# Transposed input read from memory, and the first three weight pieces split by parts, at the head of a one-core transformer kernel

## The chip, the core and the metric

The kernel runs on one core of a Trainium2 chip. A core has a matrix engine (TensorE: its matmuls are PE in the rows, its weight loads PEld), VectorE (DVE), ScalarE (ACT), GpSimd (POOL) and SyncE (SP, which here only issues transfers), each with an instruction stream of its own that runs in order and waits on semaphores. Sixteen DMA engines move data between the memory and the core's SBUF. The metric is device microseconds (us) of one execution; lower is better.

## What is computed

Two transformer blocks over 256 tokens of 1024 features, in float32. The part that the change touches is the very beginning, the root-mean-square norm and the first projection:

```python
def rmsnorm(x, g, eps=NORM_EPS):
    xf = x.astype(jnp.float32)
    y = xf * lax.rsqrt(jnp.mean(xf * xf, axis=-1, keepdims=True) + eps)
    return (y * g.astype(jnp.float32)).astype(x.dtype)
...
        h = rmsnorm(x, norm_mix_g[i])
        u = h @ w_in[i]
        u_rwkv, u_attn, u_gate = jnp.split(u, [RWKV_COLS, RWKV_COLS + ATTN_COLS], axis=-1)
        o_a = rwkv7_time_mix(u_rwkv, rwkv_mu[i], rwkv_w0[i], rwkv_w2[i], rwkv_a0[i],
...
    w = -jax.nn.softplus(-(f32(w0) + jnp.tanh(wd) @ f32(w2))) - 0.5
```

Everything behind it (a recurrence over time, attention, the feed-forward layers, the second block) is left as it is.

## The kernel before

**Weights as a stream of pieces.** All weight matrices are cut into 231 pieces of 128 x 2048 floats (1 MB). SyncE loads piece j into `raw[j % 3]`; ScalarE rounds it to the matmul's format into `hi` (emitted by `emit_hi`, a CAST at L2649); VectorE computes the remainder `lo = raw - hi` (emitted by `emit_lo`, L3017). A product is made of three matmuls, hi times high part of the activations (L2131), hi times their low part (L2132), lo times the high part (L2133). Piece j + 3 may be loaded when `lo` of piece j is done (`next_raw`, L3623). In the first stage each piece has 8 row blocks (k) and 256 columns, so it is 48 matmuls of 128x256.

**The first norm.** `x` is loaded by tokens into `X` (four transfers of 256 KB, `load_x`, L3627). TensorE transposes it (`n_part`, L2307), VectorE multiplies by the gain `g` out of PSUM (L3093), ScalarE rounds to `HH` (L2666), VectorE forms the remainder `HL` (L3099). The division by each token's root mean square is not applied to `h`: ScalarE sums the squares (`stat`, L2677), GpSimd takes the root (`root`, L3596 to L3602), VectorE puts it on a diagonal (`diag`, L3103 and L3104), TensorE spreads it over all partitions (`n_rows`, L2320, two instructions that the trace shows as four), VectorE copies it to `RB` (L3107), and each piece's result is multiplied by `RB` when it is read from PSUM (`shift`, L3148).

**The first piece.** Piece 0 comes in two halves; `first_piece` runs its matmuls in three parts (L2159, L2160, L2165, L2169). Ahead of them TensorE runs matmuls on zeros and on the identity that compute nothing (`warm`, L2138): 8 on zeros at its start, 9 on the identity (18 in the trace) ahead of piece 0.

**Where the norm's first use ends.** The mixer that eats piece 0 needs, one after another: `RB`, the multiplication L3148 (VectorE), L2696 and L2697 (ScalarE), L3152 and L3153 (VectorE), a table load and tanh (L2701), a table load and sigmoid (L2702, ScalarE), and then matmuls with `small` (L2334 and L2335, TensorE), which stand in the middle of piece 3's matmuls. `small` (the little weights, 1 MB) and the constants from column 256 on are one semaphore, `const_in`.

**What sets the order.** A planner writes one script ahead of time: `emit` adds an instruction with its expected cost to a clock per engine, and an instruction is put behind what is expected to be ready. Each engine then runs its part of the script in that order. So another cost at the beginning can give another order later.

Of the kernel before, what the change touches and what calls it, by code (L numbers as in the profile page):

```python
# [220 lines left out]
def program(nc, ws, xin, pin, colsin, constin, smallin, rowin, out):  # L221
# [4 lines left out]
    with ExitStack() as ctx:  # L226
# [14 lines left out]
        first_raw = sem("first_piece_half_in")  # L241
        first_hi = sem("first_piece_half_hi")
        first_lo = sem("first_piece_half_lo")
# [79 lines left out]
        names = [0]  # L323

# [94 lines left out]

        BK0 = Arena(8 * 4 * S)([128, 2, 512])  # L420
# [265 lines left out]
        def first_piece(c, needs, evac):  # L686

            piece_check("w_in", 0, 0, c)
            yield from split(0)
            yield from room(1)  # L690
            sl = take()
            for part in range(3):
                cur[0] = max(cur[0], lo_due[0] if part == 2 else h_due[1, part])
                emit("first", pe=16 * 0.12, part=part, slot=sl, need=unmet(needs(4 * min(part, 1))))
                if part < 2:
                    yield "pe"
            piece_done(0, sl)
            if not evac(sl, c, NSPL):
                give(sl)
            yield "pe"  # L700
# [389 lines left out]

        class FinalNorm(Norm):
# [148 lines left out]
        nm = Norm("norm_mix_g", table=False)  # L1240
        nm.part(0, 0)
        nm.part(1, 0)
        nm.low(0, 0)
        nm.low(1, 0)
        emit("first_hi")
        nm.part(0, 1)
        nm.part(1, 1)
        emit_hi(0)
        nm.low(0, 1)
        nm.low(1, 1)  # L1250
        emit("first_lo")
        emit_lo(0)
# [429 lines left out]
        def mixers_fill(nm):  # L1682
            for p, c in enumerate(RWKV_ORDER):
                def shift(sl, c, nxt, p=p):
                    early.append((p, c, sl, cur[0]))
                    if p == 1:
                        nm.rows()
                    if p:
                        to_shift.extend(early)
                        early.clear()  # L1690
# [3 lines left out]
                if p == 0:  # L1694
                    yield from first_piece(c, nm.h_needs, shift)
                else:
                    yield from cols_piece("w_in", 0, c, "h", nm.h_needs, shift)
# [414 lines left out]
        def tensor_program(e):  # L2112
# [22 lines left out]
            def warm(sl, n, w, x):  # L2135

                for _ in range(n):
                    e.matmul(banks[sl.b][:, 0:x.shape[1]], w, x, start=True, stop=True)  # L2138

            for s in script:  # L2140
                kind = s["kind"]
                sl = s.get("slot")
                if kind == "first":
                    part = s["part"]
                    wh = hi[0][:, :].rearrange("p (k n) -> p k n", k=8)
                    wl = lo[0][:, :].rearrange("p (k n) -> p k n", k=8)
                    if part == 0:
# [3 lines left out]
                    elif part == 1:  # L2151
                        e.wait_ge(hi_ready, 1)
                    if s["need"]:
                        e.wait_ge(s["need"][0], s["need"][1])
                    if part < 2:
                        for u in range(2):
                            for k in range(4 * part, 4 * part + 4):
                                w = wh[:, k, 128 * u:128 * u + 128]
                                e.matmul(b2(sl)[:, u, :], w, HH[:, k, :], start=(u, k) == (0, 0), stop=False)  # L2159
                                e.matmul(b2(sl)[:, u, :], w, HL[:, k, :], start=False, stop=False)  # L2160
                    else:
                        e.wait_ge(first_lo, 1)
                        for u in range(2):
                            for k in range(4):
                                e.matmul(b2(sl)[:, u, :], wl[:, k, 128 * u:128 * u + 128], HH[:, k, :], start=False, stop=False)  # L2165
                        e.wait_ge(lo_ready, 1)
# [1570 lines left out]
```

## Time and profile before

| | |
|---|---|
| time, median of 3 runs | 1415.09 us (1414.96 to 1415.43) |
| the profiled execution's own time | 1415.34 us |
| its span, first to last instruction | 1413.4 us (1.9 us lie around it) |
| TensorE busy | 1406.8 us of the span |
| VectorE, ScalarE busy | 1179.5 us, 819.2 us |
| memory traffic | 246.6 MB read, 175 GB/s over the span |

Busy time is the union of an engine's instructions. The ends of matmuls are modelled, so TensorE at 100% has no gap that the profile sees, and need not be at its peak. Idle time on the other engines costs nothing unless TensorE waits for them.

### The profile page before, as it was taken

What the parts mean: (1) busy time and instruction counts of PE and PEld (TensorE: products, weight loads), DVE (VectorE), ACT (ScalarE), POOL (GpSimd) and SP (SyncE); (2) the same over time, 40 slices, a digit from 0 to 9 for tenths busy, and PEclk for the clock granted to TensorE, in tenths of its full rate; (3) what the DMA queues carried; (4) which work ended last, traced back from release to release, by engine and by line L of the source; (5) the groups of instructions that cost most, each with busy time, mean ns of one, the idle gap of its engine ahead of it and who ended that gap; (6) DMA issues with size and microseconds to landing.
All of it is one profiled execution on the core that took longest, in us unless ns stands there. A gap on an engine that the chain in (4) does not pass through costs nothing.

```text
span 1413.4 us, 22918 instructions
## 1 busy us (share of the span) xinstructions
PE 1406.8 (100%) x9197; PEld 1197.1 (85%) x9197; DVE 1179.5 (83%) x1641; ACT 819.2 (58%) x1103; POOL 26.5 (2%) x93
## 2 busy tenths in 40 slices
PE   9999999999999999999999999999999999999999
PEld 8988778888888888889878888888888887888887
DVE  6876786898877898998868988988889798688897
ACT  7735474565447555555766665555555557665562
POOL 0000000000001100000000000000000000000000
PEclk9999999999999999999999999999999999999999
DMA  8441236555554555455434555545555453355543
GB/s 335 155 151 62 101 110 208 173 185 203 194 221 179 185 203 185 173 208 192 141 118 172 185 195 187 213 169 197 200 179 197 165 177 148 112 201 195 180 177 119
DMA packets 36105, 249.12 MB, mean 176 GB/s; under 512 B 4128, under 2 KB 4256, under 8 KB 6688
## 3 DMA queue, kind: packets, MB, share of 16 engines
q1 hardware_dynamic: 35712, 247.46, 49.4%
q8 instruction: 74, 1.21, 0.4%
q14 instruction: 31, 0.25, 0.1%
q10 hardware_dynamic: 288, 0.19, 0.1%
HBM read 246.59 MB, written 1.05 MB: 175 GB/s over the span
## 4 chain that ended last, share of the span: by engine, by line
PE 97%; DMA 1%; ACT 1%; DVE 0%; issue 0%; SPq 0%; DVEq 0%; ACTq 0%
PE ps L2219 24%; PE ps L2131 16%; PE ps L2133 15%; PE ps L2132 15%; PE ps L2226 13%; PE ps L2393 2%; PE ps L2203 1%; PE ps L2207 1%; PE ps L2209 1%; DMA raw<-ws 1%; PE ps L2307 1%; PE ps L2606 1%; PE ps L2586 1%; PE ps L2595 1%; PE ps L2378 0%; ACT hi L2649 0%
## 5 line engine op out<-in xcount | busy, mean ns | idle before, releaser
L3017 DVE TENSOR_TENSOR lo<-raw,hi 128x2048 fp32r<-128x2048 f32 (+1 forms) x230 | 525.0, 2283 | 60.3 <-ACT hi L2649 57.6
L2649 ACT CAST hi<-raw 128x2048 fp32r<-128x2048 f32 (+1 forms) x230 | 439.8, 1913 | 186.6 <-PE ps L2133 118.9
L2219 PE MATMUL ps<-h,hi 128*128 128x512 f32 x1504 | 359.0, 390 | 0.0
L2219 PEld LDWEIGHTS ps<-h,hi 128*128 128x128 f32 x1504 | 276.4, 188 | 52.5
L2131 PE MATMUL ps<-hi,a 128*128 128x512 f32 x516 | 205.0, 397 | 0.0
L2133 PE MATMUL ps<-hi,a 128*128 128x512 f32 x516 | 201.4, 390 | 0.0
L2132 PE MATMUL ps<-lo,a 128*128 128x512 f32 x516 | 201.2, 390 | 0.0
L2226 PEld LDWEIGHTS ps<-h,lo 128*128 128x128 f32 x1504 | 192.2, 190 | 7.9
L2226 PE MATMUL ps<-h,lo 128*128 128x256 f32 x1504 | 194.4, 282 | 0.0
L2846 ACT COPY a<-ps 128x256 f32<-128x256 f32 x208 | 76.1, 373 | 143.5 <-PE ps L2219 78.5
L2131 PEld LDWEIGHTS ps<-hi,a 128*128 128x128 f32 x516 | 96.9, 188 | 22.6 <-issue 2.4
L2133 PEld LDWEIGHTS ps<-hi,a 128*128 128x128 f32 x516 | 96.9, 188 | 20.9
L2132 PEld LDWEIGHTS ps<-lo,a 128*128 128x128 f32 x516 | 97.0, 188 | 19.1
L2131 PE MATMUL ps<-hi,h 128*128 128x512 f32 x272 | 112.0, 412 | 0.0
L2133 PE MATMUL ps<-hi,h 128*128 128x512 f32 x272 | 106.3, 391 | 0.0
L2132 PE MATMUL ps<-lo,h 128*128 128x512 f32 x272 | 106.2, 390 | 0.0
L2987 DVE TENSOR_TENSOR a<-ps,a 128x256 f32<-128x256 f32 x208 | 81.9, 420 | 17.0 <-ACT a L2846 15.1
L2131 PE MATMUL ps<-h,hi 128*128 128x256 f32 x224 | 64.8, 289 | 0.9 <-DVE lo L3017 0.9
L2132 PE MATMUL ps<-h,hi 128*128 128x256 f32 x224 | 63.4, 283 | 0.0
L2133 PE MATMUL ps<-h,lo 128*128 128x256 f32 x224 | 63.4, 283 | 0.0
L2131 PEld LDWEIGHTS ps<-hi,h 128*128 128x128 f32 x272 | 51.1, 188 | 12.2 <-issue 2.3
L2133 PEld LDWEIGHTS ps<-hi,h 128*128 128x128 f32 x272 | 51.0, 188 | 11.2
(383 smaller groups left out, 1800.1 us busy)
## 6 DMA issues: line engine op xcount, KB each, us to landing
raw<-ws SPq DMA_DIRECT2D x229, 1024.0 KB, 4.8
X<-xin SPq DMA_DIRECT2D x8, 256.0 KB, 5.3
raw<-ws SPq DMA_DIRECT2D x2, 512.0 KB, 6.5
out<-X SPq DMA_DIRECT2D x4, 256.0 KB, 2.2
small<-small SPq DMA_DIRECT2D x1, 992.5 KB, 12.8
const<-const SPq DMA_DIRECT2D x1, 900.0 KB, 6.8
a<-row SPq DMA_DIRECT2D x1, 512.0 KB, 6.2
const<-const SPq DMA_DIRECT2D x1, 388.0 KB, 13.2
```

The costliest lines, as they stand in the source:

```text
L2131: e.matmul(o, ah, bh, start=start, stop=False)
L2132: e.matmul(o, ah, bl, start=False, stop=False)
L2133: return e.matmul(o, al, bh, start=False, stop=stop)
L2203: t = e.matmul(b2(sl), wh[:, k, a:a + 128], h2[:, k, :, :], start=k == 0, stop=False)
L2207: t = e.matmul(b2(sl)[:, 0, :], wl[:, k, a:a + 128], HH[:, k, :], start=False, stop=hi_first and k == 7)
L2219: t = e.matmul(b2(s["slots"][u]), wh[:, k, 128 * u:128 * u + 128], h2[:, k, :, :], start=k == 0, stop=last)
L2226: t = e.matmul(b2(s["slots"][u])[:, 0, :], wl[:, k, 128 * u:128 * u + 128], HH[:, k, :], start=False, stop=last)
L2393: t = e.matmul(banks[z.b][half(q ^ n), 64 * h:64 * h + 64], TB[blk][l][half(q), h, :], TB[blk][r][half(q), h, :], start=True, stop=True)
L2649: e.copy(hi[j % NSPL][:, n], raw[j % NRAW][:, n]).then_inc(hi_ready, 1)
L2846: e.copy(half_to[s["to"]][s["j"]][:, s["u"], :], b2(sl)[:, 1, :]).then_inc(half_a.sem, 1)
L2987: e.tensor_tensor(to[:, u, :], b2(x)[:, 0, :], half_to[kind][j][:, u, :], ALU.add).then_inc(free[x.b], 1)
L3017: e.tensor_tensor(lo[j % NSPL][:, n], raw[j % NRAW][:, n], hi[j % NSPL][:, n].bitcast(F), ALU.subtract).then_inc(lo_ready, 1)
```

## The change

x is also loaded by features: the host gives a second array `xtin`, 128 partitions by 8 columns of gain and 8 x 256 values of x turned, and SyncE loads it in four parts into `XG`, each ahead of a quarter of piece 0. With it, ScalarE forms `HH` as x times gain (two ACTIVATE of 128x256 a part) and VectorE `HL` (two SCALAR_TENSOR_TENSOR a part), without TensorE; the transposes, the nine identity matmuls and the chain over PSUM are gone. Piece 0 is rounded in four quarters, pieces 1 and 2 in two halves, and the three of them are multiplied part by part (`FIRST`). `X` by tokens is still loaded, behind piece 1; it now serves only the sums of squares and the residual. `small` and the constants are loaded behind the issue of piece 5, and the attention tables behind that of piece 8.

```diff
-        nm = Norm("norm_mix_g", table=False)
-        nm.part(0, 0)
...
-        emit_hi(1)
-        nm.stat(0, 0)
-        nm.stat(1, 0)
-        emit_lo(1)
-        nm.stat(0, 1)
-        nm.stat(1, 1)
+        nm = FirstNorm("norm_mix_g", table=False)
+        for c in range(4):
+            emit("x_hi", act=0.9, c=c, v=part_hi.add())
+            nm.hi_at.append(part_hi.n)
+            if c < 3:
+                emit("f_hi", act=0.6, n=c, v=part_hi.add())
+            else:
+                emit_hi(0)
+            emit("x_lo", dve=0.9, c=c, v_hi=nm.hi_at[c], v=part_lo.add())
+            nm.lo_at.append(part_lo.n)
+            if c < 3:
+                emit("f_lo", dve=0.7, n=c, v_hi=part_hi.n, v=part_lo.add())
+            else:
+                emit_lo(0)
...
+        emit("f_hi", act=1.0, n=3, v=part_hi.add())
+        emit_hi(1)
+        emit("f_lo", dve=1.2, n=3, v_hi=part_hi.n, v=part_lo.add())
+        emit_lo(1)
+        for h in range(2):
+            for b in range(2):
+                nm.stat(b, h)
+        emit("f_hi", act=1.0, n=4, v=part_hi.add())
+        emit_hi(2)
+        emit("f_lo", dve=1.2, n=4, v_hi=part_hi.n, v=part_lo.add())
+        emit_lo(2)
         nm.root()
         nm.diag()
-        emit_hi(2)
-        emit_lo(2)
+        hi_part = [(part_hi.sem, n) for n in (2, 4, 6)]
+        x_part = [(part_lo.sem, n) for n in nm.lo_at]
+        FIRST = [
+            [("hi", 0, 2, [hi_part[0], x_part[0]]), ("hi", 2, 4, [hi_part[1], x_part[1]]), ("lo", 0, 2, []),
+             ("hi", 4, 6, [hi_part[2], x_part[2]]), ("lo", 2, 4, []), ("hi", 6, 8, [(hi_ready, 1), x_part[3]]),
+             ("lo", 4, 6, []), ("lo", 6, 8, [(lo_ready, 1)])],
...
-                    if p == 1:
-                        nm.rows()
-                    if p:
+                    if p > 1:
...
+                if p < 3:
+                    def known():
+                        nm.rows()
...
+                    yield from first_piece(p, c, shift, known if p == 2 else None)
...
-                        warm(sl, 9, ident, ident)
-                        e.wait_ge(first_hi, 1)
...
+                        if s["i"] == 0:
+                            e.wait_ge(zeroed, 1)
+                            warm(sl, 8, zeros[:, 0:128], zeros).then_inc(warmed, 1)
...
+                    for k in (2 * s["c"], 2 * s["c"] + 1):
+                        t = e.activation(HH[:, k, :], XT[:, k, :], ACT.Copy, scale=XG[:, k:k + 1])
+                    t.then_inc(part_hi.sem, 1)
...
+                    for k in (2 * s["c"], 2 * s["c"] + 1):
+                        t = e.scalar_tensor_tensor(HL[:, k, :], XT[:, k, :], XG[:, k:k + 1], HH[:, k, :].bitcast(F), ALU.mult,
+                                                   ALU.subtract)
+                    t.then_inc(part_lo.sem, 1)
...
                 elif kind == "lo":
                     next_raw(s["j"])
                     if s["j"] == 2:
+                        e.dma_start(small[:, :], smallin).then_inc(const_in, 16)
+                        e.dma_start(const[:, 256:late], constin[:, 256:late]).then_inc(const_in, 16)
+                    elif s["j"] == 5:
                         e.dma_start(const[:, late:NK], constin[:, late:NK]).then_inc(tables_in, 16)
```

Three places show how instructions move. First, SyncE's queue from the program's start before the change (`raw_49`, `raw_50`, `raw_51` are the three buffers of pieces 0, 1, 2 and again of 3, 4, 5):

```order
L3627 DMA X<-xin 128x512 x4
L3639 DMA raw_49<-ws 128x1024
L3640 DMA raw_49<-ws 128x1024
L3640 DMA raw_50<-ws 128x2048
L3640 DMA raw_51<-ws 128x2048
L3642 DMA small<-small 128x1985
L3643 DMA const<-const 128x776
L3623 DMA raw_49<-ws 128x2048
L3623 DMA raw_50<-ws 128x2048
```

And with the change, from the last quarter of piece 0 on (ahead of these rows stand the four parts of `xtin` and three quarters of piece 0, by turns):

```order
L3697 DMA raw_49<-ws 128x512
L3695 DMA raw_50<-ws 128x1024
L3697 DMA raw_50<-ws 128x1024
L3677 DMA X<-xin 128x512 x4
L3695 DMA raw_51<-ws 128x1024
L3697 DMA raw_51<-ws 128x1024
L3673 DMA raw_49<-ws 128x2048
L3673 DMA raw_50<-ws 128x2048
L3673 DMA raw_51<-ws 128x2048
L3701 DMA small<-small 128x1985
L3702 DMA const<-const 128x776
```

`X` moved from the front to behind piece 1, and `small` and the constants from ahead of piece 3 to behind piece 5.

Second, VectorE from the low parts of piece 1 (`lo_56`) to those of piece 3 (`lo_55`), before:

```order
L3017 TENSOR_TENSOR lo_56<-raw_50,hi_53 128x2048
L3103 TENSOR_SCALAR nt_66<-const,st 128x128
L3104 TENSOR_SCALAR nt_66<-const,st 128x128
L3017 TENSOR_TENSOR lo_57<-raw_51,hi_54 128x2048
L3138 MEMSET a_68 128x2
L3139 MEMSET a_69 128x2
L3141 TENSOR_SCALAR st<-cols 128x14
L3142 TENSOR_SCALAR st<-cols 128x4
L3143 TENSOR_SCALAR st<-cols 128x4
L3107 COPY RB<-ps 128x256
L3148 TENSOR_TENSOR a_68<-ps,RB 128x2x256
L3017 TENSOR_TENSOR lo_55<-raw_49,hi_52 128x2048
```

and with the change, from the low parts of piece 2 on:

```order
L3124 TENSOR_TENSOR lo_57<-raw_51,hi_54 128x1024
L3057 TENSOR_TENSOR lo_57<-raw_51,hi_54 128x1024
L3153 TENSOR_SCALAR nt_66<-const,st 128x128
L3154 TENSOR_SCALAR nt_66<-const,st 128x128
L3188 MEMSET a_68 128x2
L3189 MEMSET a_69 128x2
L3191 TENSOR_SCALAR st<-cols 128x14
L3192 TENSOR_SCALAR st<-cols 128x4
L3193 TENSOR_SCALAR st<-cols 128x4
L3157 COPY RB<-ps 128x256
L3057 TENSOR_TENSOR lo_55<-raw_49,hi_52 128x2048
L3198 TENSOR_TENSOR a_68<-ps,RB 128x2x256
```

The diagonal (L3103 before, L3153 now) moved from ahead of piece 2's low parts to behind them, and the first multiplication by `RB` (L3148 before, L3198 now) from ahead of piece 3's low parts to behind them.

Third, TensorE at the first use of `small`, in piece 3 (`hi_52`, `lo_55`), before:

```order
L2131 MATMUL ps<-h,hi_52 128x256
L2132 MATMUL ps<-h,hi_52 128x256
L2133 MATMUL ps<-h,lo_55 128x256
L2334 MATMUL ps<-a_67,small 128x256
L2335 MATMUL ps<-a_67,small 128x256
```

and with the change:

```order
L2171 MATMUL ps<-h,hi_52 128x256
L2172 MATMUL ps<-h,hi_52 128x256
L2173 MATMUL ps<-h,lo_55 128x256
L2365 MATMUL ps<-a_67,small 128x256
L2366 MATMUL ps<-a_67,small 128x256
```

The neighbours are the same, but ahead of the first L2334 stood 12 matmuls of piece 3, and ahead of the first L2365 stand 24. `n_rows` stands between pieces 1 and 2 on TensorE before and after. From piece 3 to some 170 us later the order differs on all three computing engines, with the same instructions; in that stretch TensorE goes from weight pieces to the mixer's small matmuls 41 times before and 39 times after. Behind it all four orders are the same as before.

## Rows read from the trace of the kernel before

**Rows 1.** The page's head: busy time by engine (share of the span).

```profile
PE 1406.8 (100%) x9197; PEld 1197.1 (85%) x9197; DVE 1179.5 (83%) x1641; ACT 819.2 (58%) x1103; POOL 26.5 (2%) x93
```

**Rows 2.** TensorE by stretch: length, busy (matmuls), granted clock, DMA share, GB/s.

```profile
1.44:9.80 8.36, 8.06 (x42) 1.00 0.94 318
9.80:23.00 13.20, 12.32 (x101) 1.00 0.95 397
31.00:205.00 174.00, 174.00 (x2520) 1.00 0.34 120
205.00:1400.00 1195.00, 1194.66 (x6433) 1.00 0.52 181
```

**Rows 3.** Timeline of TensorE, first 31 us: start, us, instruction, [idle before].

```profile
1.44 3.78 PE L2138 MATMUL ps<-lo 128*128 128x512 f32 x8 [1.44 <-DVE lo L3022]
5.02 2.48 PE L2307 MATMUL ps<-const,X 128*128 128x128 f32 x16
9.81 0.39 PE L2159 MATMUL ps<-h,hi 128*128 128x256 f32 x1 [0.30 <-ACT hi L2660]
22.63 0.61 PE L2320 MATMUL ps<-nt,const 128*128 128x128 f32 x4
23.00 0.36 PE L2131 MATMUL ps<-h,hi 128*128 128x256 f32 x1
30.67 0.45 PE L2334 MATMUL ps<-a,small 64*128 64x256 f32 x1 [0.23 <-ACT a L2702]
```

**Rows 4.** Timeline, SyncE's issues: start, time until the last of them is issued.

```profile
0.72 1.80 SPq L3627 DMA_DIRECT2D X<-xin  x4
5.14 0.43 SPq L3643 DMA_DIRECT2D const<-const  x1
13.90 9.24 SPq L3623 DMA_DIRECT2D raw<-ws  x3
```

**Rows 5.** Landings: X; pieces 0 (second half), 1, 2; pieces 3, 4; constants.

```profile
DMA to landing us min/median/max: 3.8/4.3/4.6
L3640 SPq DMA_DIRECT2D raw<-ws x3: 432/432/522, 3.0 to 4.1; - x3
DMA to landing us min/median/max: 6.9/8.8/10.9
DMA to landing us min/median/max: 7.6/7.8/8.0
const<-const SPq DMA_DIRECT2D x1, 388.0 KB, 13.2
```

**Rows 6.** Timeline of ScalarE and VectorE, the instructions that recur.

```profile
10.70 1.05 ACT L2649 CAST hi<-raw 128x1024 fp32r<-128x1024 f32 x1
12.66 1.22 DVE L3017 TENSOR_TENSOR lo<-raw,hi 128x1024 fp32r<-128x1024 f32 x1
14.30 0.58 ACT L2677 ACTIVATE ps<-X 128x512 f32<-128x512 f32 x1
17.29 0.19 ACT L2677 ACTIVATION_READ_ACCUMULATOR ps<-X 128x1 f32 x1
20.11 0.29 DVE L3103 TENSOR_SCALAR nt<-const,st 128x128 f32<-128x128 f32 x1 [3.39 <-POOL st L3582]
20.50 2.29 DVE L3017 TENSOR_TENSOR lo<-raw,hi 128x2048 fp32r<-128x2048 f32 x1
23.81 0.69 DVE L3148 TENSOR_TENSOR a<-ps,RB 128x512 f32<-128x512 f32 x1
24.35 1.92 ACT L2649 CAST hi<-raw 128x2048 fp32r<-128x2048 f32 x1 [0.52 <-DMA raw<-ws]
27.11 0.48 DVE L3152 SCALAR_TENSOR_TENSOR a<-a,cols,a 128x256 f32<-128x256 f32 x1 [0.41 <-ACT a L2697]
28.39 0.42 ACT L2701 ACTIVATE a<-a 64x256 f32<-64x256 f32 x1
```

**Rows 7.** The chain that ended last: 30 matmuls L2219 of 128x512, in mid-kernel.

```profile
267.93 6.83 PE ps L2219 x30
```

More of the change, by code:

```diff
@@ L240, in program @@
         out_done = sem("out_done")
-        first_raw = sem("first_piece_half_in")
-        first_hi = sem("first_piece_half_hi")
-        first_lo = sem("first_piece_half_lo")
+        xt_in = [sem(f"x_turned_in{c}") for c in range(4)]
+        part_in = [sem(f"piece_part_in{n}") for n in range(5)]
+        part_hi = Sig(sem("first_parts_hi"))
+        part_lo = Sig(sem("first_parts_lo"))
+        warmed = sem("warmed")
         hi_ready = sem("hi_ready")
@@ L323, in program @@
         names = [0]
+        LAST_AT = (3 * PIECE // 4, PIECE // 2, PIECE // 2)
+        PARTS_AT = [(0, slice(512 * c, 512 * c + 512)) for c in range(3)] + [(j, slice(0, PIECE // 2)) for j in (1, 2)]
         class Arena:
@@ L417, in program @@
         YT = BT[:, :, :, :].rearrange("p c b n -> p c (b n)")
+        XG = Arena(low)([128, 8 + 8 * S])
+        XT = XG[:, 8:].rearrange("p (k n) -> p k n", k=8)
         BK0 = Arena(8 * 4 * S)([128, 2, 512])
@@ L684, in piece_done, with first_piece @@
             emit_hi(i + NSPL)
-        def first_piece(c, needs, evac):
+        def first_piece(i, c, evac, between=None):
             piece_check("w_in", 0, 0, c)
-            yield from split(0)
+            yield from split(i)
             yield from room(1)
+            if between:
+                between()
             sl = take()
[L692 to L695, printed above, removed]
+            for n, (which, k0, k1, waits) in enumerate(FIRST[i]):
+                emit("first", pe=(k1 - k0) * (0.48 if which == "hi" else 0.24) * (1 if i else 1.4), i=i, which=which, k0=k0, k1=k1, slot=sl, waits=waits,
+                     opens=n == 0, closes=n == len(FIRST[i]) - 1)
+                if n < len(FIRST[i]) - 1:
                     yield "pe"
-            piece_done(0, sl)
-            if not evac(sl, c, NSPL):
+            piece_done(i, sl)
+            if not evac(sl, c, i + NSPL):
                 give(sl)
@@ L2137, in warm @@
                 for _ in range(n):
-                    e.matmul(banks[sl.b][:, 0:x.shape[1]], w, x, start=True, stop=True)
+                    t = e.matmul(banks[sl.b][:, 0:x.shape[1]], w, x, start=True, stop=True)
+                return t
             for s in script:
@@ L2153, in tensor_program @@
-                    if s["need"]:
-                        e.wait_ge(s["need"][0], s["need"][1])
-                    if part < 2:
+                        if s["i"] == 0:
+                            e.wait_ge(zeroed, 1)
+                            warm(sl, 8, zeros[:, 0:128], zeros).then_inc(warmed, 1)
+                    for who, value in s["waits"]:
+                        e.wait_ge(who, value)
+                    for k in range(s["k0"], s["k1"]):
                         for u in range(2):
-                            for k in range(4 * part, 4 * part + 4):
+                            if s["which"] == "hi":
@@ L2158, in tensor_program @@
                                 w = wh[:, k, 128 * u:128 * u + 128]
-                                e.matmul(b2(sl)[:, u, :], w, HH[:, k, :], start=(u, k) == (0, 0), stop=False)
+                                e.matmul(b2(sl)[:, u, :], w, HH[:, k, :], start=s["opens"] and (u, k) == (0, 0), stop=False)
                                 e.matmul(b2(sl)[:, u, :], w, HL[:, k, :], start=False, stop=False)
[L2161 to L2166, printed above, removed]
-                        for u in range(2):
-                            for k in range(4, 8):
+                            else:
@@ L3629, in sync_program @@
             late = KA["strict"][0]
-            for h in range(2):
-                for b in range(2):
-                    load_x(b, h)
             for s in script:
```

108 lines of the change are left out of this document (64 added, 44 removed).

## The prediction

> **What bounds the kernel now.** I read the head of the page first: TensorE is busy for 1406.8 of 1413.4 us [rows 1], so a change elsewhere counts only where TensorE waits, or where its own work goes. The stretches say where that is [rows 2]: from 31 to 205 us it does not wait at all, from 205 to 1400 us for 0.3 us. What is left is the head. There the timeline shows what TensorE does [rows 3]: matmuls on zeros from 1.44 us, the sixteen transposes from 5.02, then the identity, the first matmul that counts at 9.81, `n_rows` at 22.63, piece 2 from 23.00, the first use of `small` at 30.67 after a wait of 0.23. Between 23.00 and 30.67 it ran the 48 matmuls of piece 2 and 12 of piece 3: (30.67 - 0.23 - 23.00) / 60 = 0.124 us each. Pieces 0 and 1 are 96 x 0.124 = 11.9 us, yet piece 2 starts at 23.00, so some 11 us of the head are preparation. The gain can only come from there, and it is the distance by which TensorE is ahead at the first point from which it never waits again.
>
> **The transfers.** `X` is issued from 0.72 us on, and its first part lands at 0.72 + 3.8 = 4.5 [rows 4, 5]. Piece 0 is complete at 3.05 + 6.9 = 10.0, piece 2 at 4.1 + 10.9 = 15.0; the median of the three, piece 1, lies between, near 12.5: 2.5 us for each MB. The constants land at 5.14 + 13.2 = 18.3, piece 3 at 13.90 + 8.0 = 21.9, and that MB took 3.6 us. Piece 4 is waited for until 24.35 [rows 6], 2.4 us after piece 3.
>
> With the change the first 2 MB in the queue are turned x and piece 0 by turns. Early end: 4.5 for the first part and seven more at 2.5 us per MB, so 9.0. Late end: as the first 2 MB now, 10.0. Then piece 1 at 11.5 or 12.5, `X` at 14.0 or 15.0, piece 2 at 16.5 or 17.5, and piece 3 at 19.0 (2.5 more) or 21.1 (3.6 more, as now). Its buffer is free in time: the low parts of piece 0 end some two casts behind its landing. Piece 4 follows 2.4 later, 21.4 or 23.5.
>
> **What is removed from TensorE.** The transposes (5.02 to about 7.4) and the identity matmuls: none of it is saved as such, since TensorE would wait for data there.
>
> **The new first chunk.** The operations on `XG` are in no row of before. From below they cost ScalarE and VectorE nothing extra, because the casts and low parts of the transposed path go; from above a part costs VectorE two instructions like L3152, 2 x 0.48, and a quarter of piece 0's low part, half of 1.22: 1.6 us a part, 6.4 us for four. From the first landing at 4.5, and ScalarE's 1 us ahead of it, that ends at 11.9, and 12 matmuls after it piece 0 is done near 13.4, piece 1 near 19.4. I take this upper value, because `L3152` is the same operation on the same shape. It is covered by what follows.
>
> **The first gate: `n_rows`, between pieces 1 and 2.** On ScalarE the second half of piece 1 is cast by its landing + 1.05: 12.6 or 13.6 [rows 6]. Behind it stand the four sums of squares, 14.30 to 17.48 now, so 3.2 us: 15.8 or 16.8; `X` is there in time. Then two half casts of piece 2, 2.1 us: 17.9 or 18.9. VectorE's second half of low parts needs 1.2 more: 19.1 or 20.1. The diagonal stands behind it now, and the root is ready earlier: from 17.48 to 20.11 it takes 2.6 us, so 18.4 or 19.4. Here the moved order costs 0.7 us that it did not cost before. The diagonal takes from 20.11 to 20.50 and a handover, 0.5; `n_rows` 0.37, from 22.63 to 23.00 [rows 3]. Piece 2 starts at 20.0 or 21.0 instead of 23.00: ahead by **3.0 or 2.0 us**. TensorE, done with piece 1 near 19.4 at the latest, waits there; before it did not.
>
> **The second gate: the first use of `small`.** TensorE reaches it 72 matmuls later, 8.9 us: at 28.9 or 29.9. What it waits for is a chain that begins with piece 3, because the multiplication by `RB` now stands behind piece 3's low parts: landing, cast 1.9, low parts 2.3, L3148 0.7, piece 4's low parts 2.3 (its cast is ready by then: 21.4 or 23.5 plus 1.9), the two additions 1.0, and from tanh to the matmul 30.67 - 28.39 = 2.3: 10.5 us in all [rows 3, 6], so 29.5 or 31.6. By then 12 more matmuls are done than at 30.67 before, 1.5 us of work, so the same point lies at 32.2 in the kernel before. Ahead by **2.7 or 0.6 us**. Both ends of this gate are the smaller of the two, so it decides. Between 0.6 and 2.7 nothing in the rows is nearer: piece 3's landing was slow once (3.6 us), with the next transfer in flight, as it will be again, but it has 0.35 MB less ahead of it. I take the middle, **1.7 us**.
>
> **`small` and the constants**, moved behind piece 5, are 1.4 MB. Piece 5 is issued when piece 2's low parts end (19.1 or 20.1) and lands 2.5 behind piece 4, at 23.9 or 26.0. Now the two took from 15.0 to 18.3, so 3.3: they land at 27.2 or 29.3, and the gate needs them at 29.5 or 31.6. That is free, covered by the chain by 2.3 us; without the cover each us late costs one. The attention tables and the moved `cols` are free too: their users come much later.
>
> **The new order up to 205 us.** It holds the same instructions, and 39 changes between pieces and small matmuls instead of 41. From below zero, since the planner's order before left TensorE no wait in 174 us [rows 2]; from above unknown, a rival. I take zero.
>
> **Sum.** The profiled execution: 1415.34 - 1.7 = 1413.6 us. It lies 0.25 above the median of the runs shown, 1415.09, so I give 1413.4.
>
> **A rule that speaks against it.** Rows first: eight matmuls on zeros of 128x512 take 3.78 us at the start, 0.47 each [rows 3], thirty of the same size in mid-kernel 6.83 us, 0.23 each [rows 7]. The start ran at half rate, the lower of the clock's two levels (1.2 against 2.4 GHz), though the stretches print a granted clock of 1.00 there too [rows 2]; at 9.81 and later the rate was full, after transposes and identity had kept TensorE busy for 8.06 of 8.36 us. The Trainium skill (TensorE: Matmul & The Clock Gate, section "What's actually happening") says that the array starts at the lower level and that sustained activity releases it. By that rule the change, which takes the filler away and lets TensorE wait for parts, could hold the clock down; by the rows that I have, the eight matmuls on zeros may be enough. That is the rival on the other side.
>
> **The rivals.**
>
> *More.* Piece 3 lands at the quick end and the second gate comes no later than the first, with some gain from two fewer changes of kind: 2.7 to 3.5 us ahead, 1411.6 to 1412.4. For it: 2.5 us per MB in pieces 1 and 2. Against it: the 3.6 of piece 3.
>
> *Nothing to speak of.* Sixteen smaller issues and parts with rows of 2 KB make the transfers slower than both ends, and the second gate eats what the first gave: 0 to 0.6 us, 1414.5 to 1415.1.
>
> *The new order waits.* The planner's costs do not fit the new head, and TensorE waits inside the 174 us where it waited for nothing: 2 to 4 us there cost the gain and up to 2 more, 1415.1 to 1417.1.
>
> *The clock stays down: slower.* Pieces 0 and 1 at the lower level: first matmul at about 6.4 (first part 4.5, ScalarE and VectorE 1 us each), 96 matmuls at twice 0.124, 23.8 us, so 30.2 instead of 22.63; piece 2 at 30.6, 7.6 us late, 1422.7 us. It turns into a loss only when piece 1 ends behind 22.6: 16.2 us from 6.4, less 11.9 at full rate, leaves 4.3 us, that is 35 matmuls at the lower level (35 x 0.248 = 8.7): the clock would have to rise after 15.1 us. A rise up to about 10 us costs nothing, since piece 1 then ends by 20.0 and `n_rows` waits anyway.
>
> **How the numbers follow.** My forecast (0.6 to 2.7 us ahead, 1412.4 to 1414.5) gets 0.56, more 0.18, nothing 0.13, the order 0.07, the clock 0.06. A measurement of this kernel tells about 0.2%, 2.8 us, from no change: faster means below 1412.3, slower above 1417.9. Most of "more" is below that: faster 0.17. The forecast, nothing, and nearly all of the order case are within: 0.76. Slower is the clock and the order's tail, 0.07. The range 1411.8 to 1415.5 holds the forecast, nothing, most of more and a little of the order case, about 0.85.
>
> **What would show it.** In the changed kernel's timeline: the first L2198 near 6.4; `n_rows` (L2351) released by VectorE's diagonal between 19.6 and 20.6, with a wait of about a us ahead of it; the first L2365 released by ScalarE's sigmoid between 29.5 and 31.6, not by a transfer; no idle row of TensorE above half a us from there to 205 us; eight matmuls on zeros at 0.47 us and later ones at 0.12. I am wrong if `n_rows` comes on time and something behind 31 us waits, if the first pieces run at 0.25 us a matmul beyond 15 us, or if `const_in` releases L2365.

## The result, and the profile after

The changed kernel takes 1419.75 us (median of 10 runs, 1415.32 to 1422.19), the kernel before, beside it on the same chip, 1415.31 (10 runs, 1414.96 to 1416.07). The medians are 4.4 us apart; the ratio is 1.0026, with a 95% interval of 1.0016 to 1.0035, which is 2.3 to 5.0 us: slower, and outside the range. The ten runs fall apart: three lie at 1415.3 to 1415.8, seven at 1418.9 to 1422.2. The one with a profile took 1421.15, and what follows is read from it.

The page's head of the changed kernel, to compare with [rows 1]:

```profile
span 1419.4 us, 22865 instructions
PE 1407.7 (99%) x9163; PEld 1197.4 (84%) x9163; DVE 1178.2 (83%) x1645; ACT 819.9 (58%) x1111; POOL 28.2 (2%) x93
```

The span grew by 6.0 us and TensorE's busy time by 0.9, with 34 recorded matmuls fewer. So TensorE waits more. Its six longest waits (what for, us in total, times, longest):

```profile
PE ps L2424 <- issue: 3.2, 1, 3.2
PE ps L2178 <- DVE lo L3062: 1.4, 1, 1.4
PE ps L2198 <- ACT hi L2693: 1.4, 1, 1.4
PE ps L2424 <- DVE a L3278: 0.8, 1, 0.8
PE ps L2365 <- ACT a L2740: 0.5, 1, 0.5
PE ps L2351 <- DVE nt L3154: 0.3, 1, 0.3
```

Four of these belong to the head. L2424, the mixer's small matmuls of 64x64, did not wait before. The places of the prediction first, in TensorE's timeline (start, length, instruction, idle time ahead of it and what ended it), which answers to [rows 3]:

```profile
1.44 3.78 PE L2178 MATMUL ps<-lo 128*128 128x512 f32 x8 [1.44 <-DVE lo L3062]
6.58 0.58 PE L2198 MATMUL ps<-h,hi 128*128 128x256 f32 x1 [1.37 <-ACT hi L2693]
...
21.86 0.68 PE L2351 MATMUL ps<-nt,const 128*128 128x128 f32 x4 [0.31 <-DVE nt L3154]
22.30 0.36 PE L2198 MATMUL ps<-h,hi 128*128 128x256 f32 x1
...
31.65 0.45 PE L2365 MATMUL ps<-a,small 64*128 64x256 f32 x1 [0.49 <-ACT a L2740]
```

Piece 2 starts at 22.30 instead of 23.00, and the first use of `small` at 31.65 is released by ScalarE, not by a transfer. There 24 matmuls of piece 3 are done against 12 before, a point that the prediction put at 32.2 for the kernel before: 0.5 us ahead. The same timeline 60 us later:

```profile
92.35 0.40 PE L2173 MATMUL ps<-hi,h 128*128 128x512 f32 x1
93.53 1.16 PE L2424 MATMUL ps<-a,a 64*64 64x64 f32 x64 [0.78 <-DVE a L3278]
94.63 0.66 PE L2381 MATMUL ps<-const,a 128*128 128x128 f32 x4
95.21 1.04 PE L2424 MATMUL ps<-a,a 64*64 64x64 f32 x54
99.49 0.58 PE L2424 MATMUL ps<-a,a 64*64 64x64 f32 x10 [3.24 <-issue]
100.00 2.07 PE L2388 MATMUL ps<-a,const 128*128 128x256 f32 x4
```

In the new order two groups of 64 small matmuls stand together. Behind the 54th of the second TensorE stops for 3.24 us. The code has no wait there, and the view names none ("issue"). Behind it the long matmuls are slow, and the stretches show why (length, busy time and number by engine, granted clock, DMA share, GB/s):

```profile
96.00:99.50 3.50, 0.26 (x20) 0.12 (x10) 0.38 (x1) 0.40 (x1) 0.00 (x0) 0.85 0.78 276
99.50:105.30 5.80, 5.80 (x82) 4.46 (x81) 1.29 (x2) 1.07 (x2) 0.00 (x0) 0.50 0.17 68
105.30:110.00 4.70, 4.70 (x52) 3.76 (x56) 1.29 (x2) 2.24 (x4) 0.00 (x0) 1.00 0.00 0
```

The granted clock was at its lower level, 0.50, until 105.3. So the loss lies in one place: 0.78 us of a wait for VectorE, 3.24 without a releaser, and the lower clock behind it.

What came in the 3.24 us? The page's queues show one that carries instructions, 73 packets of 16 KB (packets, MB, share):

```profile
q8 instruction: 73, 1.20, 0.3%
```

There are 9163 matmuls and as many weight loads. If these are what the packets carry, one of them, a block from here on, is some 125 matmuls. The DMA view has none between 92.50 and 97.25 us, while weight piece 16 is on its way at up to 552 GB/s, and one between 97.25 and 98.40:

```profile
q8 instruction: 1, 0.02, 5.2%
```

The packet's record says 97.30 to 98.26. TensorE went on at 99.49, 1.23 later. My theory from here on: TensorE ran out of instructions, because the next block stood behind a weight piece. Rival A: the head itself costs it, by the lower clock up to 13 us or by late gates. Rival B: a wait of the new order for data.

### The profile page after: what moved, and what is told of

It reads as the page before. It is cut to its first block, busy times and chain, and to the rows that moved or that the text cites. A ratio compares the mean times of both kernels' runs of the same rounds, so it can differ in the third digit from the quotient of the medians.

```text
span 1419.4 us, 22865 instructions
## 1 busy us (share of the span) xinstructions
PE 1407.7 (99%) x9163; PEld 1197.4 (84%) x9163; DVE 1178.2 (83%) x1645; ACT 819.9 (58%) x1111; POOL 28.2 (2%) x93
## 4 chain that ended last, share of the span: by engine, by line
PE 96%; DMA 1%; DVE 1%; ACT 1%; issue 0%; SPq 0%; DVEq 0%; ACTq 0%
PE ps L2252 24%; PE ps L2171 16%; PE ps L2173 15%; PE ps L2172 15%; PE ps L2259 13%; PE ps L2424 2%; PE ps L2236 1%; PE ps L2240 1%; PE ps L2242 1%; DMA raw<-ws 1%; PE ps L2336 1%; PE ps L2637 1%; PE ps L2617 1%; PE ps L2626 1%; DVE lo L3057 0%
## 5 line engine op out<-in xcount | busy, mean ns | idle before, releaser
L2259 PE MATMUL ps<-h,lo 128*128 128x256 f32 x1504 | 194.4, 282 | 0.0
L2172 PEld LDWEIGHTS ps<-lo,h 128*128 128x128 f32 x272 | 51.4, 189 | 8.7
L2171 PE MATMUL ps<-h,hi 128*128 128x256 f32 x192 | 55.4, 289 | 0.0
L2704 ACT CAST h<-nt 128x512 fp32r<-128x512 f32 x32 | 19.8, 620 | 61.4 <-DVE nt L3139 61.1
```

Of the source, the lines that this page charges most:

```text
L2171: e.matmul(o, ah, bh, start=start, stop=False)
L2172: e.matmul(o, ah, bl, start=False, stop=False)
L2259: t = e.matmul(b2(s["slots"][u])[:, 0, :], wl[:, k, 128 * u:128 * u + 128], HH[:, k, :], start=False, stop=last)
L2704: e.copy(HH[:, 4 * h:4 * h + 4, 128 * b:128 * b + 128], n4[s["n"] % 2]).then_inc(h_hi.sem, 1)
```

## Experiments

Each was timed beside the kernel before, whose median was 1415.2 to 1415.4 in each; the time given is the median of 11 runs, of 5 in g2_border_back.

**Head and order apart.** The planner's due times are set back at the first `n_rows`, so that nearly all behind piece 10 is ordered as before:

```
  nm.rows()
+ due.update(pe=31.6, act=31.0, dve=32.05)
+ cur[0] = due['pe']
```

> The head of the change with the planner's due times set back at the first n_rows, so that from piece 10 on the order of every engine is that of before. Theory (the 3.24 us gap and the fall of the granted clock behind it come from the new order at 85 to 100 us, where TensorE's next block of instructions stands behind weight pieces): no idle row of TensorE above 1 us between 23 and 205 us, granted clock at the upper level throughout from 13 us on, 1414.3 to 1415.3 us, the 0.5 us that the gates put the kernel ahead. Rival A (the head itself costs it: the lower clock up to 13.1 us, late gates): 1418.5 to 1420 us as measured for the change. Rival B (a wait of the new order for data): 1414.3 to 1415.3 us as well, so this run tells A from the other two.

Measured: 1414.65 us (1414.28 to 1415.44), ratio 0.9996 (0.9988 to 1.0005). TensorE's last 8900 matmuls have the shapes and the order of before. Behind 23 us TensorE waits 0.3 us for X at L2345 and for nothing else. The head is not what costs: it gives some 0.6 us by the ratio, though the interval reaches past no change, and 0.5 in the profiled runs. Its largest wait is at `n_rows`:

```profile
21.97 0.46 PE L2353 MATMUL ps<-nt,const 128*128 128x128 f32 x2 [1.62 <-DVE nt L3156]
```

The other half, the head of before with due times of the change (38.15, 38 and 41) set behind its first `n_rows`:

> The head of before, all loads as before, with the planner's due times set at the first n_rows so that nearly all the order behind it is that of the changed kernel (4046 of 4150 rows of TensorE alike at the end). Theory (blocks of instructions): a gap of some 2 to 3 us without a releaser in or near the two groups of 64 small matmuls at 93 to 99 us if the block's border falls there too (the head of before has some 68 more TensorE instructions, so the border comes 68 instructions earlier and the gap is shorter or absent, at the least 0 us): 1415.3 to 1420 us. Rival A (the head): 1415.0 to 1415.6 us, no gap. Rival B (a wait of the new order for data, whatever the blocks): the gap at the same group with the same 3.2 us, 1418.5 to 1420 us.

Measured: 1416.34 us (1415.90 to 1416.63), ratio 1.0007 (0.9998 to 1.0016). The order is that of the changed kernel for the last 8900 matmuls. No gap, but two waits for VectorE in it:

```profile
93.73 1.16 PE L2395 MATMUL ps<-a,a 64*64 64x64 f32 x64 [0.79 <-DVE a L3230]
94.82 0.65 PE L2352 MATMUL ps<-const,a 128*128 128x128 f32 x4
95.41 1.16 PE L2395 MATMUL ps<-a,a 64*64 64x64 f32 x64
...
98.72 1.00 PE L2395 MATMUL ps<-a,a 64*64 64x64 f32 x53 [0.40 <-DVE a L3210]
```

So rival B is a true part, 1.0 us by the medians (the interval just reaches no change), and the rest needs order and head together.

**The border of the block.** Four of the changed kernel's warm-up matmuls are replaced by 64 small ones, so every border falls 60 matmuls earlier in the program:

```
- warm(sl, 8, zeros[:, 0:128], zeros).then_inc(warmed, 1)
+ for _ in range(64):
+     e.matmul(banks[sl.b][0:64, 0:64], zeros[0:64, 0:64], zeros[0:64, 0:64], start=True, stop=True)
+ warm(sl, 4, zeros[:, 0:128], zeros).then_inc(warmed, 1)
```

> The changed kernel with 4 of the 8 warm-up matmuls on zeros replaced by 64 small ones (64x64): 120 more TensorE instructions ahead of everything, order and loads unchanged, so each border of a 256-instruction block falls 120 instructions earlier in the program. Theory (blocks): the block that came at 97.30 us is asked for while TensorE still works on long matmuls and lands by 94 us; no gap above 1 us at 93 to 100 us, clock at the upper level there, 1414.5 to 1416 us. Rival A (head) and rival B (a wait for data): the gap of 3.2 us stays and the time with it, 1418.5 to 1421 us.

Measured: 1417.87 us (1416.58 to 1418.83), ratio 1.0017. The gap is gone from its place, as the theory says and both rivals deny, but the time missed its range. The new warm-up is longer, 7.03 us, which leaves the kernel 0.9 behind the changed one at 42 us, and two other borders now lie inside groups of small matmuls:

```profile
106.48 0.56 PE L2426 MATMUL ps<-a,a 64*64 64x64 f32 x21
107.36 0.91 PE L2426 MATMUL ps<-a,a 64*64 64x64 f32 x43 [0.31 <-issue]
...
115.59 1.03 PE L2426 MATMUL ps<-a,a 64*64 64x64 f32 x53
117.00 0.44 PE L2426 MATMUL ps<-a,a 64*64 64x64 f32 x11 [0.37 <-issue]
```

Counted from the end of the program, the gap of the changed kernel stands ahead of matmul 8190. These stand ahead of 8000 and 7751: 8190 + 60 = 8250, less two and four blocks of 125, is 8000 and 7750. So the blocks do carry TensorE's instructions, some 125 matmuls each.

With 34 more records instead of 60, where the head of before has its border:

```
- warm(sl, 8, zeros[:, 0:128], zeros).then_inc(warmed, 1)
+ for n in range(18):
+     c = half(n % 2)
+     e.matmul(banks[sl.b][c, 0:64], zeros[c, 0:64].bitcast(F), zeros[c, 0:64].bitcast(F), start=True, stop=True)
+ warm(sl, 6, zeros[:, 0:128], zeros).then_inc(warmed, 1)
```

> The changed kernel with 34 more TensorE matmul records in the warm-up (2 of its 8 large matmuls replaced by 18 small ones that are recorded twice each), so that the border falls where e2_new_order has it. Theory: no gap above 0.8 us at 93 to 100 us, only the 1.2 us of waits for VectorE in the new order stay: 1415.3 to 1416.5 us. Rival A (the head costs it): 1418.5 to 1421 us. With 60 more records (e3_block_border) the borders had moved to two later groups and 1417.87 us were left.

Measured: 1416.84 us (1416.13 to 1419.24), ratio 1.0012. No gap at 93 to 100 us. The median is 0.3 above the range, for something else: in the profiled run `n_rows` waited 2.37 us and the clock was at its lower level from 21.5 to 24.9.

And the gap brought into the head of before, by 34 matmuls fewer in it. For that piece 0's chunk leaves out nearly all its low products, and more than half of those with the low part of h:

```
- warm(sl, 9, ident, ident)
+ warm(sl, 4, ident, const[:, 0:256])
...
- e.matmul(b2(sl)[:, u, :], w, HL[:, k, :], start=False, stop=False)
+ if part == 0 and (u, k) != (0, 3):
+     e.matmul(b2(sl)[:, u, :], w, HL[:, k, :], start=False, stop=False)
...
- for u in range(2):
-     for k in range(4, 8):
+ for u in (1,):
+     for k in (7,):
```

> As e2_new_order (head of before, order of the changed kernel, 1416.34 us), with 34 fewer TensorE instruction pairs in the head, so that the border of the block falls at the same matmul as in the changed kernel; piece 0's first chunk leaves out most of its low products for that. Theory (border and piece on its way together make the gap): the gap of some 3 us is back behind the 54th matmul of the second group of 64, and in most runs the lower clock behind it, 1418.5 to 1421.5 us. Rival A (the gap belongs to the head of the change) and rival B (it belongs to the order alone): as e2_new_order, no gap there, 1415.5 to 1416.6 us.

Measured: 1423.63 us (1420.92 to 1424.00), ratio 1.0053 (1.0040 to 1.0065), 2.1 above the range. The head loses 2 us that it should not (TensorE, with less work, waits 2.4 us for a low part of the next piece, and the granted clock is 0.50 from 15.0 to 21.8 us), and the gap is back at the same matmul and as long, with the clock down from 100.3 to 107.1:

```profile
97.48 1.04 PE L2393 MATMUL ps<-a,a 64*64 64x64 f32 x54
101.75 0.69 PE L2393 MATMUL ps<-a,a 64*64 64x64 f32 x10 [3.24 <-issue]
```

**The piece in the way.** The changed kernel, but only a quarter of piece 16 loaded:

```
- e.dma_start(raw[i][:, :], ws[j + NRAW]).then_inc(raw_in[i], 16)
+ n = slice(0, PIECE // 4 if j + NRAW == 16 else PIECE)
+ e.dma_start(raw[i][:, n], ws[j + NRAW][:, n]).then_inc(raw_in[i], 16)
```

> The changed kernel with three quarters of weight piece 16 not loaded (its rest keeps the numbers of an earlier piece): the piece that is on its way from 92.7 to 97.3 us. Theory (the block of instructions waits until the piece is drained): the block comes at 93.6 to 94.5 us instead of 97.30 and the gap of 3.24 us is under 1 us, clock at the upper level, 1414.5 to 1416 us. Rival A (head): unchanged, 1418.5 to 1421 us. Rival B (a wait for data of the new order): unchanged as well, since piece 16 is not what the small matmuls read.

Measured: 1416.45 us (1415.35 to 1417.38), ratio 1.0008. The gap shrank to 1.10 us, as against both rivals, but all three figures of the theory were missed a little: the block began at 95.15, the gap is above 1 us, the time 0.45 above the range. And with 16 columns of it instead of 512:

```
+ n = slice(0, 16 if j + NRAW == 16 else PIECE)
```

> The changed kernel with all but 16 columns of weight piece 16 not loaded, so that hardly anything is on its way from 92.7 to 97 us. Theory (the block of instructions whose border TensorE meets behind the 54th matmul of the second group was asked for at 92 to 93.5 us and waited for the piece to drain): the block comes by 94.2 us, and as TensorE went on 1.2 to 1.4 us behind the landing in the three gaps seen, the gap is 0 to 0.5 us instead of 3.24 (1.10 with a quarter of the piece); 1414.8 to 1416.2 us. Rival (TensorE always stops some 1 us at such a border, whatever is on its way): gap 1.0 to 1.3 us as with a quarter of the piece, 1416 to 1417 us.

Measured: 1416.07 us (1415.33 to 1416.97), ratio 1.0007. The row behind the 54th matmul, first with a quarter of the piece, then with next to nothing:

```profile
97.33 0.39 PE L2424 MATMUL ps<-a,a 64*64 64x64 f32 x10 [1.10 <-issue]
```

```profile
96.75 0.39 PE L2424 MATMUL ps<-a,a 64*64 64x64 f32 x10 [0.73 <-issue]
```

The blocks came at 95.15 to 96.08 and 94.19 to 95.51. TensorE went on 1.25 and 1.24 us behind the landing. So the piece is worth 3.24 - 0.73 = 2.5 us. My 0 to 0.5 was too low: 0.7 are left when hardly anything is in the way. The rival's 1.0 to 1.3 fails as well, though it has this part in kind. What the 0.7 come from is argued only: TensorE crossed the border before, 125 matmuls earlier, at 91.66 and had used up its block by 96.02, 4.4 us, and the next one's first matmul came 5.1 us behind that border.

**The clock of the head.** As e1_old_order, with a longer warm-up:

```
- warm(sl, 8, zeros[:, 0:128], zeros).then_inc(warmed, 1)
+ warm(sl, 11, zeros[:, 0:128], zeros).then_inc(warmed, 1)
```

> The head of the change with the order of before behind it (as e1_old_order, 1414.65 us), and 11 warm-up matmuls on zeros instead of 8, so that TensorE is busy until its first weights come at 6.6 us. Theory (in the head the n_rows gate is set by the diagonal that VectorE makes, so the clock costs nothing there; the change lost only in the new order): the granted clock rises by 7 us instead of 10.3, TensorE waits 1.6 to 3.5 us longer for n_rows, 1414.3 to 1415.0 us, no difference from e1_old_order above 0.4 us. Rival A (the low clock of the head is what it costs): 1.5 to 3 us less than e1_old_order, 1411.5 to 1413.2 us.

Measured: 1415.81 us (1414.48 to 1416.54), ratio 1.0001 (0.9992 to 1.0010): 1.2 above e1_old_order, outside either range, and opposite to rival A. The clock had risen by 7.06 us (0.12 us a matmul from there on), TensorE waited longer for `n_rows`, as expected, and then the clock fell:

```profile
22.19 0.68 PE L2353 MATMUL ps<-nt,const 128*128 128x128 f32 x4 [2.19 <-DVE nt L3156]
```

```profile
22.30:23.60 1.30, 1.30 (x12) 1.30 (x13) 0.42 (x1) 1.30 (x1) 0.00 (x0) 1.00 0.85 340
23.60:27.00 3.40, 3.40 (x18) 3.40 (x18) 3.28 (x3) 2.28 (x3) 0.00 (x0) 0.50 1.00 419
```

The eleven runs lie in two groups, five at 1414.5 to 1414.9, within the theory's range, and six at 1415.8 to 1416.5; the mean granted clock was 1.000 in four of the five and 0.999 in all six. So the miss goes with the fall of the clock, and an earlier clock ahead of a gate that holds was worth nothing. Nor is the early rise due to the 11 matmuls alone: with 8, it had come by 7.3 us in the profiled runs of e4_short_piece, f1_rows_behind_part, f2_lora_early, g1_no_piece and h1_diag_ahead.

**The gates.** On top of e1_old_order, in three steps, with TensorE's due time set back to 33.4 instead of 31.6; the order of TensorE's last 8900 matmuls stays that of before. First `n_rows` behind the first part of piece 2:

```
- if between:
-     between()
  sl = take()
  for n, (which, k0, k1, waits) in enumerate(FIRST[i]):
+     if between and n == 1:
+         between()
```

> As e1_old_order, and n_rows of the first norm is put behind the first part of piece 2 instead of ahead of it. Theory (the wait of 1.62 us at n_rows is order, since the first part of piece 2 is ready at 19 us): that wait is gone, TensorE comes to the first use of small at 32.5 us instead of 34.1 and waits there for ScalarE's sigmoid, which in e1_old_order was done at 33.85; so 0.2 us of the 1.6 are kept: 1414.2 to 1414.8 us. Rival (the second gate does not hold, all of it is kept): 1412.8 to 1413.2 us.

Measured: 1414.00 us (1412.76 to 1415.29), ratio 0.9992 (0.9983 to 1.0001). The second gate holds as expected (0.20 us for ScalarE's sigmoid), the time came 0.2 below the range. Then entries of piece 0's chain moved ahead in the finished script, `ahead` putting the first entry of one kind in front of another:

```
+ ahead({"kind": "shift"}, {"kind": "lo", "j": 3})
+ ahead({"kind": "shift_old"}, {"kind": "hi", "j": 4})
+ ahead({"kind": "shift_add"}, {"kind": "lo", "j": 4})
+ ahead({"kind": "lora_in"}, {"kind": "hi", "j": 5})
```

> As f1_rows_behind_part, and VectorE's and ScalarE's steps of piece 0 up to tanh and sigmoid (shift, shift_old, shift_add, lora_in) put ahead of the halves of pieces 3, 4 and 5. Theory (the second gate is the chain of small steps behind the halves of weights; with them ahead it opens at 30.2 to 31.6 us, before TensorE comes there at 32.5): the wait at the first use of small is gone, 1412.8 to 1413.5 us. Rival (ScalarE, busy without a break from 28 to 48 us in e1_old_order, is what sets the stretch behind): 1414.2 to 1414.8 us, with the wait further back.

Measured: 1413.61 us (1412.62 to 1415.32), ratio 0.9989 (0.9980 to 0.9998). No wait at the second gate and none further back; 0.1 above the range. Last, 11 warm-up matmuls and piece 3 by halves (`p < 4` where `first_piece` is chosen):

```
  FIRST = [
  ...
+     [(w, k, k + 4, [(r, 4)] if k == 0 else []) for w, r in (("hi", hi_ready), ("lo", lo_ready)) for k in range(0, 8, 4)],
```

> As f2_lora_early, with 11 warm-up matmuls and piece 3 taken high half first and low half behind it, as pieces 1 and 2. Theory (now nothing but data bounds TensorE in the head: piece 2's last part at 20.6 us and piece 3's low half at about 26 us): TensorE is at the first use of small by 30.5 us, 3.5 us ahead of e1_old_order, 1411.0 to 1412.3 us. Rival (ScalarE's steps or the loads bound the stretch from 28 to 48 us): as f2_lora_early or above, 1413 to 1414.8 us.

Measured: 1412.92 us (1412.19 to 1413.92), ratio 0.9983 (0.9974 to 0.9992): between the two. The first use of `small` came at 32.23 instead of 30.5, and from 9.04 us on TensorE waited only 0.29 us, at `n_rows`, so it was mostly its own work that set the head. The step changes two things at once, and what each is worth was not told apart: in the profile of f2_lora_early the granted clock was 0.50 from 8.8 to 12.3 us, in this one it did not fall.

**The root.** That `n_rows` came at 21.9 in all of these had a cause of its own. GpSimd (POOL) in the changed kernel, and VectorE beside it:

```profile
17.68 0.71 POOL L3628 TENSOR_TENSOR st<-st 128x2 f32<-128x2 f32 x1
18.46 0.86 POOL L3629 TENSOR_TENSOR st<-st 128x2 f32<-128x2 f32 x1
19.40 1.13 POOL L3630 TENSOR_TENSOR st<-st 128x2 f32<-128x2 f32 x1
20.62 0.19 POOL L3631 TENSOR_SCALAR st<-st 128x2 f32<-128x2 f32 x1
```

```profile
18.04 1.23 DVE L3124 TENSOR_TENSOR lo<-raw,hi 128x1024 fp32r<-128x1024 f32 x1 [2.88 <-ACT hi L2693]
19.25 1.23 DVE L3057 TENSOR_TENSOR lo<-raw,hi 128x1024 fp32r<-128x1024 f32 x1
21.23 0.29 DVE L3153 TENSOR_SCALAR nt<-const,st 128x128 f32<-128x128 f32 x1 [0.75 <-POOL st L3632]
```

In the kernel before, whose VectorE stood still then, the same two steps (L3579 and L3580 there) took 0.20 each, while the one ahead of them (L3628, L3578 there) took 0.71 in both:

```profile
18.97 0.20 POOL L3579 TENSOR_TENSOR st<-st 128x2 f32<-128x2 f32 x1
19.24 0.20 POOL L3580 TENSOR_TENSOR st<-st 128x2 f32<-128x2 f32 x1
```

With the change each ends just behind the low part that ran beside it (18.04 + 1.23 = 19.27, 19.25 + 1.23 = 20.48). The edit, on e1_old_order and on f3_full_head:

```
+ nm.root()
+ nm.diag()
  emit("f_lo", dve=1.2, n=4, v_hi=part_hi.n, v=part_lo.add())
  emit_lo(2)
- nm.root()
- nm.diag()
```

> As e1_old_order (1414.65 us), and GpSimd's root and VectorE's diagonal put ahead of VectorE's two low parts of piece 2 (TensorE's, ScalarE's and SyncE's order unchanged). Theory (in the new head those low parts, 18.1 to 20.6 us, run beside GpSimd's root and hold it up: two of its steps take 0.86 and 1.13 us in the changed kernel where they took 0.20 in the kernel before, whose VectorE stood still then): the two steps take 0.20 us again, the diagonal begins near 19.8 us instead of 21.3, n_rows comes by 20.6 us instead of 21.97 with a wait under 0.4 us. The second gate, the sigmoid at 33.85, does not move, so TensorE waits there for about 1 us and the time falls by 0.2 to 0.4 us only: 1414.2 to 1414.5 us. Rival (GpSimd's steps are slow for a reason of their own): n_rows at 21.9 us as before, 1414.6 us.

Measured: 1413.56 us (1413.09 to 1414.61), ratio 0.9989 (0.9981 to 0.9998). The two steps take 0.19 us, the diagonal begins at 19.68, `n_rows` does not wait:

```profile
18.50 0.19 POOL L3631 TENSOR_TENSOR st<-st 128x2 f32<-128x2 f32 x1
18.77 0.19 POOL L3632 TENSOR_TENSOR st<-st 128x2 f32<-128x2 f32 x1
```

The gain of 1.1 us was more than I allowed: TensorE came to the second gate at 33.10 and found it open, since the chain behind the diagonal moved too (the sigmoid was done at 32.87 instead of 33.85).

> As f3_full_head (1412.92 us), with the same step ahead. There n_rows waited 0.29 us and the rest of the head is TensorE's own work from 9.04 us on. Theory: the 0.29 us go, 1412.4 to 1412.8 us, if piece 2's low parts, ready at 22.9 us instead of 20.6, still come ahead of TensorE (it asks for them at 24 us). Rival: the low parts come late and take it back, 1412.9 to 1413.5 us.

Measured: 1412.36 us (1411.72 to 1414.04), ratio 0.9981 (0.9972 to 0.9990), 2.8 us below the kernel before: the best of all, and just under the theory's range. What holds it at the second gate is now a transfer, for 0.2 us:

```profile
PE ps L2368 <- DMA const<-const: 0.2, 1, 0.2
```

## Why the prediction was wrong

**"The new order up to 205 us ... I take zero"** is the step that failed. The rows of before showed no wait in 174 us, and I took that for a property of the work. It was one of that order with that head. At the same matmul (6500 from the end of the program, at 205.37 us in the changed kernel and 199.21 before) the changed kernel is 6.2 us late, though 0.5 ahead at 31.65. Of the 6.7 us between, 0.78 are the wait for VectorE and 3.24 the block. The lower clock is 2.5: the work from 99.49 to the long matmul at 105.20 took 5.7 us; in g1_no_piece the same matmuls took from 96.75 to 100.39 at the upper level, 3.6, of which 0.4 were a wait for VectorE that the changed kernel does not have there, so 3.2. 0.2 stay unplaced. The rival *The new order waits* had the place, and 2 to 4 us for what came to over 6; its mechanism (costs that do not fit the new head) covers the 0.78 only.

Shown by runs: head without order does not lose (e1_old_order), order without the border loses 1.0 (e2_new_order), the gap moves with the border (e3_block_border, g3_border_away) and comes back with it in the other head (g2_border_back), and its length follows the piece on its way (e4_short_piece, g1_no_piece). That the lower clock follows from the gap is read from the two profiles with a 3.24 us gap, and from none with a shorter one at that place. Not shown is what the three runs of the changed kernel at 1415.3 to 1415.8 did: none of them has a profile. But their mean granted clock is on record, 1.000, 1.000 and 0.999 against 0.996 to 0.999 in the seven others. And the profiled run falls back by 5.6 us on e2_new_order between the matmul ahead of the gap and matmul 8100 (counted from the end); without that it would have taken 1421.15 - 5.6 = 1415.6 us, an estimate that lies among the three. So gap and low clock were probably both absent from them; why the gap should come in most executions and not in all stays open.

**The first gate** was mis-sized. "The root is ready earlier ... it takes 2.6 us": it took from 17.12 to 21.09, 4.0 us, against VectorE's low parts, and piece 2 started at 22.30 instead of 20.0 or 21.0, ahead by 0.7 instead of 3.0 or 2.0. Of the 1.3 us behind the late end, 0.75 are VectorE's wait for the root, and 0.4 came with the transfers: the second half of piece 2 was cast when it landed, at 18.10, 0.6 behind the late end for it, and its low parts ended at 20.48 for 19.1 or 20.1. `n_rows` waited 0.31 us and not about one, since TensorE came there at 21.55 instead of 19.4, with the clock at its lower level until 13.1 us (in e1_old_order, where the rate was full from 10.4 on, the wait was 1.62).

**The second gate** was right in kind, the sigmoid released it at 31.65 for "29.5 or 31.6". Its late end gives 0.6 ahead, 0.5 was measured, and the middle, 1.7, was the wrong choice; e1_old_order puts the head's worth at 0.7 by the medians. But the chain that set it began with piece 4, not with piece 3. The casts of the two on ScalarE, and the low parts of piece 4 on VectorE:

```profile
20.59 1.90 ACT L2680 CAST hi<-raw 128x2048 fp32r<-128x2048 f32 x1 [1.44 <-DMA raw<-ws]
24.31 1.91 ACT L2680 CAST hi<-raw 128x2048 fp32r<-128x2048 f32 x1 [1.82 <-DMA raw<-ws]
26.25 2.29 DVE L3057 TENSOR_TENSOR lo<-raw,hi 128x2048 fp32r<-128x2048 f32 x1 [0.25 <-ACT hi L2680]
```

Piece 3 landed at 20.6, within "19.0 or 21.1"; its low parts began at 23.11, 0.6 behind their cast, since the late `RB` stood ahead of them. Piece 4 landed at 24.3 for "21.4 or 23.5", and VectorE, which was to find its cast ready, waited for it. That the sum met its late end within 0.1 us is in part luck.

**`small` and the constants** were free as predicted, with less cover: the constants, issued at 22.13 and 8.0 us on their way, were in near 30.1 for "27.2 or 29.3". `const_in` released nothing until h2_full_head_diag.

***The clock stays down*** was right in its sum: first matmul at 6.58 for 6.4, clock up at 13.1 us, later than 10 and sooner than 15.1, and no loss in the head. The 13.1 belongs to one execution, as the 10.4 of e1_old_order with the same head shows. I looked for the clock at the start alone; it cost 2.5 us some 85 us later, around a wait.

## What to carry to other kernels

Where a planner orders the work, a change at the head is a new order for all behind it: hold the old order fixed, and price head and order apart. In this kernel long rows of 64x64 matmuls used up their instructions before the next block came, by 0.7 us with hardly any transfer on its way and by 3.2 with one of 1 MB; a wait that has no releaser in the middle of such a row is a reason to look at the instruction queue. GpSimd's small steps were held up by a neighbour that the timeline shows only beside them: compare the same line's duration before and after.

## What the runs showed of the hardware

**Instructions on the road.** The gap of 3.24 us, 1.10 with a quarter of the piece and 0.73 without it, is the wait for one 16 KB block; from its landing to the next matmul 1.23 to 1.25 us passed in these three, and 1.57 in g2_border_back. The Trainium skill (Runtime: NRT & Kernel Launch, section "Instruction fetch mechanics") has blocks of 16 KiB, 256 instructions, whose crossing is mostly hidden. The size agrees with the 73 packets; the hiding does not hold at this border, and the measurement decides.

**GpSimd beside VectorE.** Steps of 0.20 us took 0.86 and 1.13 beside low parts that read two tensors, and 0.19 again once these stood elsewhere. The Trainium skill (SBUF — State Buffer, section "SBUF: two separate sides") describes a port that the two engines share as an exclusive lock, where a VectorE instruction with two SBUF inputs blocks a GpSimd one that reads SBUF to its end. The runs agree with it for GpSimd's waits. The other way about they show nothing of it: the low part that began at 18.04, while GpSimd's L3628 ran from 17.68 to 18.39, took 1.23 us as the next one did.

**The clock falls in mid-kernel.** The level went down with waits of 3.24 us (twice), 2.19 and 2.37: 1.0 us ahead of the end of the wait in the changed kernel, 1.5 in g2_border_back, 0.4 in g3_border_away, and 1.4 behind it in e5_longer_warm. In the gaps of 0.73 and 1.10 it stayed up. It also went down inside the head of six other profiled runs: between 7.8 and 9.3 us in e4_short_piece, f1_rows_behind_part, f2_lora_early, g1_no_piece and h1_diag_ahead, around two waits of 1.4 to 2.0 and 0.6 to 1.0 us, and at 15.0 us in g2_border_back, within a wait of 2.41 that followed one of 1.00. In h2_full_head_diag it stayed up with two waits of 1.06 and 1.09, so the length of a single wait does not settle it. The changed kernel's low level until 13.1 us is not printed by the stretches (1.00 there); the matmuls' spacing shows it, 0.21 us up to there and 0.12 behind.
